# A bias table reversed early and read backwards, later cache loads and four gate banks in a four-layer diffusion step

## The reference

```python
row_b = (row_idx - r[:, None]) + (WIN_ROWS - 1)
col_b = jnp.clip(ck[None, :] - cq[:, None] + (WIN_COLS - 1), 0, 2 * WIN_COLS - 2)
bias = rpb[:, row_b[:, None, :, None], col_b[None, :, None, :]].astype(jnp.float32)
s_loc = jnp.einsum('brqhd,brkwhd->bhrqkw', q, kg).astype(jnp.float32) * ATTN_SCALE + bias[None]
s_loc = jnp.where(valid_col[:, None, :], s_loc, -jnp.inf)
s_ctx = jnp.einsum('brqhd,bmhd->bhrqm', q, ctx_k).astype(jnp.float32) * ATTN_SCALE
...
x = x + g1 * m
h = rms_norm(x, norm2_g[i]) * (1 + sc2) + sh2
x = x + g2 * moe(h, router_w, router_b, moe_w_gate[i], moe_w_up[i], moe_w_down[i])
```

## Time and profile before

| | before |
|---|---|
| median of 3 runs | 1340.72 us (1338.42 to 1341.14) |
| the profiled execution's own time | 1340.35 us |
| its span in the profile | 1338.5 us |
| busy TensorE (PE) | 1257.5 us, 94% |
| busy VectorE (DVE), ScalarE (ACT), GpSimd (POOL) | 391.2, 327.5, 38.8 us |
| moved by DMA | 535.14 MB, mean 400 GB/s |
| chain that ended last | PE 76%, DMA 17%, DVE 4%, ACT 1% |

### The profile page before, as it was taken

One profiled execution on the slowest core, in us unless ns is written; L12 is line 12 of the kernel. 1 busy time (PEld: TensorE's weight loads), 2 busy tenths in 40 slices (PEclk: granted clock), 3 DMA queues, 4 the chain that ended last, 5 costly groups with the idle time before them and its releaser, 6 DMA issues.

```text
span 1338.5 us, 18150 instructions
## 1 busy us (share of the span) xinstructions
PE 1257.5 (94%) x6589; PEld 565.9 (42%) x6589; DVE 391.2 (29%) x884; ACT 327.5 (24%) x706; POOL 38.8 (3%) x76
## 2 busy tenths in 40 slices
PE   3878999999899999999999898999999899999996
PEld 0434434343756644443433254443443354434342
DVE  1242213223132324221331324221331453213314
ACT  1231212122121223221221223221221352212222
POOL 3010000000100000100000000000000000000000
PEclk9889999999999999999999999999999999999998
DMA  9999999999999889899999999899999999999995
GB/s 372 420 418 422 421 420 422 422 421 420 341 410 402 345 347 364 346 409 420 422 422 422 421 409 411 313 408 420 422 422 422 415 421 375 414 420 423 421 422 225
DMA packets 87261, 535.14 MB, mean 400 GB/s; under 512 B 11193, under 2 KB 13337, under 8 KB 25761
## 3 DMA queue, kind: packets, MB, share of 16 engines
q1 hardware_dynamic: 82336, 527.47, 96.4%
q0 software_dynamic: 3120, 5.17, 1.2%
q10 hardware_dynamic: 1744, 1.73, 0.4%
HBM read 532.20 MB, written 2.12 MB: 399 GB/s over the span
## 4 chain that ended last, share of the span: by engine, by line
PE 76%; DMA 17%; DVE 4%; ACT 1%; issue 1%; SPq 0%; DVEq 0%; ACTq 0%
PE ps L1890 27%; PE ps L1939 13%; DMA ring<-in_ada_w_dram 7%; DMA ring<-in_moe_w_up_dram 5%; PE ps L1876 5%; PE ps L1428 4%; PE ps L1577 4%; PE ps L1951 4%; PE ps L1541 4%; DMA ring<-in_moe_w_down_dram 3%; PE ps L1586 2%; PE ps L1922 2%; DMA xh<-in_moe_w_up_dram 2%; PE ps L1513 1%; PE ps L1907 1%; DVE hT L986 1%
## 5 line engine op out<-in xcount | busy, mean ns | idle before, releaser
L1890 PE MATMUL ps<-ring,xg 128*64 128x512 f32 x968 | 440.1, 597 | 8.5 <-DMA ring<-in_moe_w_up_dram 7.6
L1892 PE MATMUL ps<-ring,xg 128*64 128x512 f32 x944 | 430.2, 598 | 0.0
L1939 PE MATMUL ps<-ring,gb 128*64 128x512 f32 x992 | 227.7, 596 | 1.5 <-DMA ring<-in_moe_w_down_dram 1.4
L1890 PEld LDWEIGHTS ps<-ring,xg 128*64 128x64 f32 x968 | 123.8, 136 | 244.4 <-issue 231.5
L1352 DVE SCALAR_TENSOR_TENSOR gb<-ps,gslot,g2x 128x512 f32<-128x512 f32 x128 | 90.2, 747 | 254.4 <-PE ps L1939 254.4
L1939 PEld LDWEIGHTS ps<-ring,gb 128*64 128x64 f32 x992 | 68.4, 137 | 135.6 <-issue 119.0
L1892 PEld LDWEIGHTS ps<-ring,xg 128*64 128x64 f32 x944 | 121.0, 137 | 0.0
L871 ACT ACTIVATE y_hi<-gb 128x512 fp32r<-128x512 f32 x128 | 77.2, 626 | 172.5 <-PE ps L1951 108.7
L1428 PE MATMUL ps<-ring,cact 128*32 128x512 f32 x768 | 96.0, 635 | 13.6 <-DMA ring<-in_ada_w_dram 8.2
L858 ACT ACTIVATE gu<-ps 128x512 f32<-128x512 f32 x64 | 38.3, 598 | 209.6 <-PE ps L1892 209.6
L1361 DVE TENSOR_TENSOR y_lo<-gb,y_hi 128x512 fp32r<-128x512 f32 x128 | 83.6, 689 | 12.9 <-ACT y_hi L871 12.3
(11 more groups left out here) (213 smaller groups left out, 1102.7 us busy)
## 6 DMA issues: line engine op xcount, KB each, us to landing
ring<-in_moe_w_down_dram SPq DMA_DIRECT2D x124, 1024.0 KB, 17.6
ring<-in_moe_w_gate_dram SPq DMA_DIRECT2D x121, 1024.0 KB, 17.1
ring<-in_moe_w_up_dram SPq DMA_DIRECT2D x118, 1024.0 KB, 17.5
ring<-in_ada_w_dram SPq DMA_DIRECT2D x96, 1024.0 KB, 17.9
ring<-in_attn_wqkv_dram SPq DMA_DIRECT2D x12, 1024.0 KB, 20.8
spare<-in_moe_w_gate_dram SPq DMA_DIRECT2D x4, 1024.0 KB, 18.6
xh<-in_moe_w_up_dram SPq DMA_DIRECT2D x4, 1024.0 KB, 18.7
hT<-in_moe_w_down_dram SPq DMA_DIRECT2D x4, 1024.0 KB, 20.0
```

The costliest lines, as they stand in the source:

```text
L1890: mg = pe.matmul(ps[0:SLOTS, B_GU, :], xg[:, b, e, :], wg[:, i * F:(i + 1) * F], start=(b == 0), stop=(b == DB - 1))
L1892: mu = pe.matmul(ps[SLOTS:P, B_GU, :], xg[:, b, e, :], wu[:, i * F:(i + 1) * F], start=(b == 0), stop=(b == DB - 1))
L1939: mm = pe.matmul(ps[r * SLOTS:(r + 1) * SLOTS, DOWN_BANKS[e % 2], :], acts[:, e % ACTS, j, :], w[:, i * D + r * HALF:i * D + (r + 1) * HAL ...
```

## The change

The table is laid out the other way round. `rpad` now has the 31 column differences on partitions and the heads innermost, [128, 3, 16]; three DMAs read it with single numbers of 4 bytes, since the heads lie far apart in the input. `kattn` is loaded ahead of it, at the start of the program, and its permutation now reverses all 128 rows. In layer 0, between norm 1 and the mixer, TensorE reverses the table with one matmul (`backwards`), VectorE copies it to `rback`, and POOL writes it to `bias_rows` [3, 128, 16]. `braw` is then read in runs of 64 columns x 16 heads, and VectorE makes the bias straight from `braw`, with the steps through the keys going backwards. The four flips and their banks go. `ck` and `cv` are fetched one norm later (`s_ms` 3, which is norm 1 of layer 1). The second gates are one matmul of 64 rows in layers 0 and 3, and in layers 1 and 2 two matmuls of 32 rows that each fill all partitions of a bank of their own; each copy to `g2x` becomes two of 64 partitions.

```diff
-GATE_BANKS = [[(0, 1, 2), (0, 1, 1)], [(0, 1, 6), (0, 1, 7)], [(0, 1, 2), (0, 1, 2)], [(0, 1, 2), (0, 1, 1)]]
+GATE_BANKS = [[(0, 1, 2, 2), (0, 1, 1, 1)], [(0, 1, 6, 7), (0, 1, 2, 7)], [(0, 1, 2, 3), (0, 1, 2, 7)], [(0, 1, 2, 2), (0, 1, 1, 1)]]
...
-    attn[i, 1, (i // GRID_W) * GRID_W + GRID_W - 1 - cq] = 1.0
+    attn[i, 1, P - 1 - i] = 1.0
...
-        bias_dram = nc.dram_tensor("bias_rows", [HEADS, 3, P], F32, kind="Internal").ap()
+        bias_dram = nc.dram_tensor("bias_rows", [3, P, HEADS], F32, kind="Internal").ap()
...
-            pool.dma_start(rpad[:, :, 48:79], attn_rpb[0, :, WIN_ROWS - 2:WIN_ROWS + 1, :]).then_inc(s_bias, 16)
-            pool.wait_ge(s_bias, 16)
-            pool.dma_start(bias_dram, rpad[:, :, :]).then_inc(s_bias, 16)
+            pool.dma_start(kattn[:, :, :].rearrange("p a t -> p (a t)"), k_attn).then_inc(s_kattn, 16)
+            for d in range(3):
+                pool.dma_start(rpad[48:79, d, :], attn_rpb[0, :, WIN_ROWS - 2 + d, :].rearrange("h i -> i h"),
+                               allow_slow_non_contiguous=True).then_inc(s_bias, 16)
+            pool.wait_ge(s_rback, 1)
+            pool.dma_start(bias_dram.rearrange("d p h -> p d h"), rback[:, :, :]).then_inc(s_bias, 16)
             for t in range(2, 4):
                 ada_bias(t)
...
-            pool.wait_ge(s_ms, 2)
-            pool.wait_ge(s_bias, 32)
+            pool.wait_ge(s_ms, 3)
+            pool.wait_ge(s_bias, 64)
             pool.dma_start(ck[:, :], cache_k[0, 0].rearrange("m h d -> m (h d)")).then_inc(s_ck, 16)
             pool.dma_start(cv[:, :], cache_v[0, 0].rearrange("m h d -> m (h d)")).then_inc(s_ck, 16)
-            pool.dma_start(kattn[:, :, :].rearrange("p a t -> p (a t)"), k_attn).then_inc(s_ck, 16)
...
-                    src = bass.AP(tensor=bias_dram.tensor, offset=(kr - r + 1) * P,
-                                  ap=[[1, GRID_W], [3 * P, HEADS], [1, GRID_W]])
-                    pool.dma_start(braw[r * GRID_W:(r + 1) * GRID_W, :, kr * GRID_W:(kr + 1) * GRID_W], src).then_inc(s_bias, 16)
+                    src = bass.AP(tensor=bias_dram.tensor, offset=((kr - r + 1) * P + 1) * HEADS,
+                                  ap=[[HEADS, GRID_W], [1, GRID_W * HEADS]])
+                    pool.dma_start(braw[r * GRID_W:(r + 1) * GRID_W, kr, :, :].rearrange("p k h -> p (k h)"), src).then_inc(s_bias, 16)
...
-                nc.scalar.activation(g2x[:, s, :], ps[:, GATE_BANKS[l][s][2], :], ACT.Copy).then_inc(s_g2x, 1)
+                for j in range(2):
+                    part = slice(64 * j, 64 * (j + 1))
+                    ins = nc.scalar.activation(g2x[part, s, :], ps[part, GATE_BANKS[l][s][2 + j], :], ACT.Copy)
+                ins.then_inc(s_g2x, 1)
...
-                v.wait_ge(s_ck, 48)
-                mask = kattn[:, 0, :].unsqueeze(1).to_broadcast([P, 4, P])
-                for b in range(4):
-                    v.wait_ge(s_job, JOB_DONE[FLIPS + b])
-                    v.scalar_tensor_tensor(bias[:, 4 * b:4 * b + 4, :], ps[:, JOB_BANK[FLIPS + b], :].rearrange("p (h k) -> p h k", h=4),
-                                           1.0 / SCALE, mask, ALU.mult, ALU.add).then_inc(s_jd, 1)
+                v.wait_ge(s_bias, 16 * 8)
+                flat = braw[:, :, :, :].rearrange("p r k h -> p (r k h)")
+                for kr in range(2):
+                    cols = slice(kr * GRID_W, (kr + 1) * GRID_W)
+                    back = bass.AP(tensor=flat.tensor, offset=flat.offset + ((kr + 1) * GRID_W - 1) * HEADS,
+                                   ap=[flat.ap[0], [1, HEADS], [-HEADS, GRID_W]])
+                    v.scalar_tensor_tensor(bias[:, :, cols], back, 1.0 / SCALE, kattn[:, 0, cols].unsqueeze(1).to_broadcast([P, HEADS, GRID_W]),
+                                           ALU.mult, ALU.add).then_inc(s_biased, 1)
+                v.wait_ge(s_biased, 2)
...
+                        v.wait_ge(s_back, 1)
+                        v.tensor_copy(rback[:, :, :].rearrange("p d h -> p (d h)"), ps[:, 7, 0:3 * HEADS]).then_inc(s_rback, 1)
...
+                    pe.matmul(ps[:, GATE_BANKS[l][s][2], :], const[64:128, C_SEL + s * P:C_SEL + (s + 1) * P], grow[64:128, l % 2, :],
+                              start=True, stop=True).then_inc(s_bc2, 1)
+                    return
...
-                pe.wait_ge(s_ck, 48)
-                pe.wait_ge(s_bias, 16 * 6)
-                flat = braw[:, :, :].rearrange("p h k -> p (h k)")
-                for b in range(4):
-                    room(FLIPS + b)
-                    mm = pe.matmul(ps[:, JOB_BANK[FLIPS + b], :], kattn[:, 1, :], flat[:, b * 512:(b + 1) * 512], start=True, stop=True)
-                    done(FLIPS + b, mm)
+                pe.wait_ge(s_ck, 32)
...
+            def backwards():
+
+                pe.wait_ge(s_kattn, 16)
+                pe.wait_ge(s_bias, 48)
+                pe.matmul(ps[:, 7, 0:3 * HEADS], kattn[:, 1, :], rpad[:, :, :].rearrange("p d h -> p (d h)"),
+                          start=True, stop=True).then_inc(s_back, 1)
...
+                    if l == 0:
+                        backwards()
+                        pe.wait_ge(s_rback, 1)
                     mixer_pool(l, base)
```

More of the change, by code:

```diff
@@ L322, in build @@
             sb("at2_hT", [P, DB, T], F32, at2)
-            braw = sb("braw", [P, HEADS, P], F32, at2)
+            braw = sb("braw", [P, 2, GRID_W, HEADS], F32, at2)
         with ExitStack() as pl:
@@ L332, in build @@
             vrow = sb("vrow", [P, P], F32, pl)
-            rpad = sb("rpad", [HEADS, 3, P], F32, pl)
+            rpad = sb("rpad", [P, 3, HEADS], F32, pl)
+            rback = sb("rback", [P, 3, HEADS], F32, pl)
         with ExitStack() as last:
@@ L410, in build @@
         s_ck = sem("s_ck")
+        s_kattn = sem("s_kattn")
+        s_back = sem("s_back")
+        s_rback = sem("s_rback")
+        s_biased = sem("s_biased")
         s_job = sem("s_job")
@@ L461, in build @@
         N_VECTOR_LOADS = 5
-        Q0, K0, FLIPS, CK_TURNS, K_TURN0, V0, Q1A, Q1B, K1A, K1B, V1A, K_TURN1, V1B = 0, 2, 4, 8, 10, 11, 13, 14, 15, 16, 17, 18, 19
-        JOBS = "adad" + "dddd" + "aaa" + "ad" + "adad" + "aad"
-        JOB_BANK = [0, 4, 5, 6, 7, 0, 4, 5, 6, 7, 0] + [4, 5] * 4 + [4]
+        Q0, K0, CK_TURNS, K_TURN0, V0, Q1A, Q1B, K1A, K1B, V1A, K_TURN1, V1B = 0, 2, 4, 6, 7, 9, 10, 11, 12, 13, 14, 15
+        JOBS = "adad" + "aaa" + "ad" + "adad" + "aad"
+        JOB_BANK = [0, 4, 5, 6, 7, 0, 4] + [5, 4] * 4 + [5]
         CLOSES = {Q0 + 1: 0, K0 + 1: 2, V0 + 1: 4, Q1B: 1, K1B: 3, V1B: 5}
@@ L1491, in second_gates @@
                 for j in range(2):
-                    rows32, cols = slice(64 + 32 * j, 96 + 32 * j), slice(64 * j, 64 * (j + 1))
-                    mm = pe.matmul(ps[cols, GATE_BANKS[l][s][2], :], const[rows32, C_SEL + s * P + 64 * j:C_SEL + s * P + 64 * (j + 1)],
+                    rows32 = slice(64 + 32 * j, 96 + 32 * j)
+                    mm = pe.matmul(ps[:, GATE_BANKS[l][s][2 + j], :], const[rows32, C_SEL + s * P:C_SEL + (s + 1) * P],
                                    grow[rows32, l % 2, :], start=True, stop=True)
@@ L1501, in gates @@
                     pe.wait_ge(s_g2x, 2 * l + 1)
+                if B_ADA in GATE_BANKS[l][s]:
+                    pe.wait_ge(s_mod, 10)
                 first_gates(l, s)
@@ L1535, in project @@
                             gates(l, 1)
-                        if cc == 1 and banks[2 * cc + s] == GATE_BANKS[l][s][2]:
-                            pe.wait_ge(s_g2x, 2 * l + s + 1)
+                        if cc == 1:
+                            pe.wait_ge(s_g2x, 2 * l + 2)
                         for h in range(2):
```

## The result

The changed kernel takes 1346.82 us (median of 7 runs, 1344.55 to 1352.29) against 1340.72 us before; the ratio is 1.0066 with a 95% interval of 1.005 to 1.0082. It is slower by 0.66% (the medians alone are 6.1 us, 0.45%, apart), and outside the range given. The profiled execution took 1349.69 us, with a span of 1347.9.

The account below looks back on a forecast made before the run. DMA bounds the kernel up to 336 us, PE from 337 to 565. Flips -3.43, queries' start -0.3 and gates +0.2 sum to -3.5 us against 1340.35: 1336.8, stated as 1337.0, range 1334.3 to 1344.5.

Parts of the forecast that it names:

- The gather: Table loads in the DMA-bound stretch: 1488 single numbers at 12.2 ns, spread over 16 engines, cost 1.1 us (bound 2.9).
- The gather's case: Rival: each table load runs on one engine, which lags and delays units up to 336 us; middle 1346 us, chance 0.22.
- Layer 0's wait: Ahead of layer 0's mixer: table lands by 25 to 30 us, before the mixer's start at 38.54; cost 0.
- TensorE's lateness is covered: Layer 0: TensorE can be some 10 us late before DMA stands idle; cost 0.
- Flips and VectorE's bias: Between keys and scores: four flips leave TensorE's stretch, -3.43 us; VectorE's bias reads, 2.6 to 5.2 us, stay hidden, 0.
- The keys' later fetch: DMA-bound stretch loses 2.6 us of ck and cv; 1.9 (0.8 to 2.6) return ahead of the queries' second unit.
- The gates: Layer 3 gains little and extra ScalarE copies cost; layers 1 and 2 lose perhaps 0.1; sum +0.2 us (0 to +0.9).

Follow-up runs that it names:

- e3: Kernel before plus three unused GpSimd loads of the same 1488 single numbers, behind the table's write; 1352.43 us, 1.0119.
- e13: Kernel before plus three unused GpSimd loads of 32 rows of 16 single numbers (1536 pieces), 64 bytes apart in the source; 1340.63 us, 1.0013.
- e7: Kernel before plus three unused GpSimd loads of the same 1488 places, each piece 64 bytes in place of one number; 1352.22 us, 1.011.
- e6: Kernel before plus one unused GpSimd load of 496 single numbers in place of three; 1343.37 us, 1.0034.
- e15: Changed kernel with each table load taking 32 rows of 16 single numbers in place of 31, same result; 1333.3 us, 0.9957 to the kernel before.
- e4: Changed kernel, but table loaded in 31-number runs, reversed by a VectorE copy, turned by three TensorE transposes; 1334.94 us, 0.997 to the kernel before.
- e5: As e4, but cached keys fetched after the second norm of layer 0, as before the change; 1336.2 us, 0.9962 to the kernel before.
- e8: As e4, but with the gates as before the change; 1336.06 us, 0.9979 to the kernel before.

## Why the prediction was wrong

**The gather, the step that failed.** The forecast had "so 1488 cost 18.2 us of one engine, 1.1 us on 16" and measured were 13.9 us. The price of a piece was near; the division by 16 was the error. The packets say so. The kernel before has this q0 on its page:

```profile
q0 software_dynamic: 3120, 5.17, 1.2%
```

e3 adds 432 packets and 0.09 MB for 5.95 KB of numbers; e13 adds 96 packets and so little that the column doesn't move. I take 48 packets in each as the ends of 3 loads on 16 engines. Then e13 has one packet left for each load and engine, 32 numbers each. e3 has 384 left, eight for each load and engine, and their sizes in the trace are 336 of 256 bytes and 48 of 192: seven of 64 numbers and one of 48, which are all 496 numbers of a load, 16 times over (16 x 5.95 KB = 0.095 MB). The changed kernel has the same 384. e7 fixes who carries the data: of its 384 packets 24 carry pieces of 64 bytes (21 of 4096 bytes, 3 of 3072), one set of eight for each load, and 360 are the small ones (315 of 256 bytes, 45 of 192), 15 sets for each load. That is 0.095 MB of data once and 0.089 MB beside it, the 0.18 MB that its page has more; sixteen copies of the data would be 1.5 MB. So with 31 rows, by these counts, one engine carries a load and the other 15 each do as many pieces of 4 bytes. That each set stands for one engine is worked out; the trace does not name engines.

1488 pieces in 13.9 us are 9.3 ns a piece on every engine, within a quarter of the 12.2 of the earlier trace rows; with 32 rows each engine has 96 pieces in place of 1488. The loss does not stand in the packets of the loads, which took 81 ns each in the median and 1.9 us of 16 engines in all in the changed kernel. It stands in the weights' packets of 8 KB beside them: from 20 to 25 us the kernel before started 244, and all took 300 to 350 ns (314 in the median); the changed kernel started 77, of which 73 took longer than 350 ns (839 in the median of all). 525 ns more for a weight packet and 81 for the loads' own, over 64 pieces, are 9.5 ns a piece. Why a small packet makes the next large one longer stays open.

**The rival.** The gather's case was the one that came true, with its condition (31 rows and 16 engines) and nearly its middle (1346). Half of its mechanism was not: one engine does carry the data of a load, but it did not lag behind the others. With one engine late, most of the weights' packets should have kept their length; 73 of 77 were longer, and the window shows 293 GB/s at full DMA share. Nor does its price fit, 6 or 15 us with the three loads side by side, each on an engine of its own: in e6's window, with 372 GB/s, one load costs 38 x 50 / 420 = 4.5 us, and three cost 13.9: in sum, not side by side.

```profile
17.00:67.00 50.00, 38.81 (x224) 17.21 (x224) 10.48 (x27) 13.19 (x26) 7.75 (x10) 0.93 1.05 372
```

The rule of the Trainium skill that the prediction weighed (DMA: Bandwidth & Descriptors, "Why a DMA increments its semaphore by 16 and not by 1": the largest number of engines up to 16 that divides the slowest dimension of both sides, one for 31) agrees with e7's packets (the data on one set of 16), with e13 and with e15 (32 rows, 1.3 us in e13); the exception that it names did not hold for these loads. I had given the rule less than a quarter.

**Layer 0's wait.** The table was to land by 25 to 30 us and landed at 52.4, as GpSimd's third issue stood for 19.54 us. TensorE's timeline of the changed kernel has the wait for it:

```profile
52.54 0.64 PE L1831 MATMUL ps<-rpad,kattn 128*128 128x48 f32 x2 [5.29 <-DMA rpad<-in_attn_rpb_dram]
```

That is 5.29 us of the 15 by which the mixer starts late; ahead of it the conditioning units were late. That TensorE's lateness is covered held, at 15 us where I had said 10: e3, in which nothing waits for the loads, loses as much as the loads lose in the changed kernel (293 GB/s both).

**Flips and VectorE's bias**: right, by e15, in which nothing of the loads is in the way. `ck` follows the keys without a gap. The two reversed reads took 3.79 us, between the 2.6 and 5.2 that I had set, and 5.02 us of idle time are left; VectorE's timeline of e15:

```profile
372.56 3.79 DVE L1115 SCALAR_TENSOR_TENSOR gb<-braw,kattn 128x1024 f32<-128x1024 f32 x2
381.36 0.42 DVE L1088 TENSOR_REDUCE r_ge<-ps 128x2 f32<-128x256 f32 x1 [5.02 <-PE ps L1628]
```

**The keys' later fetch**: dearer ahead of the queries than its bound. TensorE's timelines of the kernel before and of e15 show the last conditioning unit 2.05 us earlier in e15, but the queries 0.26 us later than in the earlier trace rows, after 5.30 us of waiting for their second unit:

```profile
336.00 1.07 PE L1428 MATMUL ps<-ring,cact 128*32 128x512 f32 x8 [1.43 <-DMA ring<-in_ada_w_dram]
```

```profile
333.95 1.06 PE L1446 MATMUL ps<-ring,cact 128*32 128x512 f32 x8 [1.44 <-DMA ring<-in_ada_w_dram]
...
342.65 29.26 PE L1601 MATMUL ps<-hT,ring 128*128 128x256 f32 x128 [5.30 <-DMA ring<-in_attn_wqkv_dram]
```

By the semaphores in the traces that unit lands 5.38 us behind the last conditioning unit before (341.34) and 8.61 us in e15 (342.52): 3.2 us lost ahead of it, where I had 1.9 and at most 2.6. e4 has 8.18 us there (2.8 lost), and e5, with the keys early, 5.39 again. What the fetch gives back ahead of the last conditioning unit is as much: that unit landed at 332.78 in e4 and at 335.85 in e5. In these executions it gains and loses about 3 us, which fits two times that can't be told apart. `ck` and `cv`, issued at 332.68 and 333.25, landed 7.0 and 8.4 us later, both ahead of it.

**The gates**: wrong in sign. I had +0.2. In layer 1 before, first and second gates ran one behind the other; TensorE's timeline of the kernel before:

```profile
493.10 1.13 PE L1482 MATMUL ps<-grow,const 32*128 32x512 f32 x4
494.16 1.07 PE L1493 MATMUL ps<-grow,const 32*64 32x512 f32 x4
495.16 3.70 PE L1541 MATMUL ps<-ring,o_first 128*128 128x512 f32 x8
```

and of e15:

```profile
488.90 0.70 PE L1500 MATMUL ps<-grow,const 32*128 32x512 f32 x2
488.91 0.70 PE L1514 MATMUL ps<-grow,const 32*128 32x512 f32 x2
489.43 0.59 PE L1500 MATMUL ps<-grow,const 32*128 32x512 f32 x2
489.44 0.59 PE L1514 MATMUL ps<-grow,const 32*128 32x512 f32 x2
489.97 3.70 PE L1565 MATMUL ps<-ring,o_first 128*128 128x512 f32 x8
```

From the first gate to the next product 2.06 us became 1.07. Before, the two matmuls of a pair already ran side by side, 0.01 us apart in the trace, and the pairs one behind the other; now all four lie side by side. Banks and shape changed together (the second pair was 32*64 in one bank and is 32*128 in two), so which of the two did it is not shown. There are four such places in layers 1 and 2: 2.06 us each before; 1.19, 1.07, 1.71 and 1.07 in e15, which saves 3.2 us in all. e4 has the same four numbers, and e8, with the old gates, has 2.06 at each again; its timeline at the place above:

```profile
488.61 1.13 PE L1499 MATMUL ps<-grow,const 32*128 32x512 f32 x4
489.67 1.07 PE L1510 MATMUL ps<-grow,const 32*64 32x512 f32 x4
490.67 3.70 PE L1558 MATMUL ps<-ring,o_first 128*128 128x512 f32 x8
```

So the gates are a term of -3.2 us on TensorE where the forecast had +0.2. With the 3.49 us at the turns of `ck` it makes 6.7 us; the profiled executions of e15 and of the kernel before are 7.05 us apart, and by the ratio e15 gains 5.8 us (0.43% of 1339.49). By time alone e4 against e8 shows no more than 1.1 us, which their intervals do not tell from nothing. In layer 3 one matmul of 64 rows did not halve the time, since there too the two of 32 rows had run side by side (1.98 us for four against 1.93 for eight, timeline of e15 against the earlier trace rows):

```profile
1083.24 1.98 PE L1507 MATMUL ps<-grow,const 64*128 64x512 f32 x4 [0.67 <-DVE grow L1015]
```

**The sum with what was measured.** With 32 rows the change is 5.8 us faster than the kernel before; loads at 13.9 us in place of 1.3 make that 6.8 us slower. The ratio says 8.8 (0.66%), the medians 6.1. So the sign of the forecast turned on the one step above; without it the change gains more than the 3.5 us that I had, and the gates are the term that I had undervalued.

## What to carry to other kernels

Before many small pieces are costed by dividing by 16 engines, look at the rows of the load: here 31 rows of 16 single numbers, three times, cost 13.9 us in a stretch that DMA bounds, and 32 rows 1.3. The packets and megabytes of a queue on the page tell it: 5.95 KB of numbers that count as 0.09 MB are, by the counts above, work that all engines do. The share of time on the same line hardly tells it (1.2% became 1.3 to 1.4), since the time is lost in the other queue's packets. A load that no one waits for is not free where DMA sets the pace.

## What the runs showed of the hardware that was not expected

Loads of 31 rows of single numbers from GpSimd's queue counted 16 times their bytes and made nearly all of the weights' packets on another queue longer (839 ns in place of 314 for 8 KB, in the median of 20 to 25 us), 9.3 ns a piece on every engine; with 32 rows the same kind of load cost a tenth. ScalarE's queue counted the same pieces once. GpSimd stood 19.54 us ahead of the third such load, ScalarE 36.88 us on its second. Four matmuls of 32 rows, each filling all partitions of a bank of its own, ran side by side in 1.07 us, where two pairs, the second in a narrower shape and in one bank, had taken 2.06.
